# Four small moves in a hybrid layer's step: sums and turns one or two steps later, seven leading steps, tanh behind the turned weights

## The reference

```python
h = rms_norm(x, lw['norm_w'])
proj = jnp.einsum('bsd,de->bse', h, lw['w_in']) + lw['b_in']
(dn_qkv, dn_z, dn_b, dn_a, lru_x, lru_g, fq, fk, fv, ff, fg, mq, mg, mgate) = jnp.split(proj, IN_OFFSETS, axis=-1)
# A: gated DeltaNet (conv, l2 norms, per-head decay dn_a, beta dn_b, chunks of 64, gated norm)
# B: RG-LRU (conv, block-diagonal gates, scan)
# C: forgetting attention: 4 heads of 128, logits + c[t] - c[s], c = cumulative sum of log forget (ff), causal
# M: cross-attention into 256 memory tokens, 4 heads of 128, with normed q and k
# each branch -> D_MODEL, times sigmoid(mgate) of that branch, summed, output projection, + x
```

## Time and profile before

| | |
|---|---|
| median of 3 runs | 1656.29 us (1655.22 to 1657.52) |
| profiled execution, own time | 1660.77 us |
| its span | 1659.1 us |
| TensorE busy | 1604.7 us (97%) |
| VectorE busy | 886.6 us (53%) |
| ScalarE busy | 537.8 us (32%) |
| GpSimd busy | 507.3 us (31%) |
| mean granted clock of TensorE | 0.994 |

### The profile page before, as it was taken

One profiled execution on the slowest core, in us unless ns is written; L12 is line 12 of the kernel. 1 busy time (PEld: TensorE's weight loads), 2 busy tenths in 40 slices (PEclk: granted clock), 3 DMA queues, 4 the chain that ended last, 5 costly groups with the idle time before them and its releaser, 6 DMA issues. The chain is left out here.

```text
span 1659.1 us, 26024 instructions
## 1 busy us (share of the span) xinstructions
PE 1604.7 (97%) x10539; PEld 1538.3 (93%) x10539; DVE 886.6 (53%) x1291; ACT 537.8 (32%) x935; POOL 507.3 (31%) x382
## 2 busy tenths in 40 slices
PE   5999999999999999999999999999999999999998
PEld 4989999999999999999889889999989999889976
DVE  4678752444444442790486772444667552895611
ACT  6323343222222222233344442311145223654300
POOL 2433416334333312811344551222212221103400
PEclk9999999999999999999999999999999999999999
DMA  4212155222222114532276353135210332434521
GB/s 157 53 26 54 52 151 133 71 58 71 71 71 71 52 52 145 154 116 78 85 191 191 112 177 102 46 121 164 60 39 17 112 103 69 150 120 143 150 90 58
DMA packets 189365, 163.16 MB, mean 98 GB/s; under 512 B 18381, under 2 KB 157056, under 8 KB 188727
## 3 DMA queue, kind: packets, MB, share of 16 engines
q1 hardware_dynamic: 189246, 161.51, 34.0%
HBM read 131.38 MB, written 30.22 MB: 97 GB/s over the span
## 5 line engine op out<-in xcount | busy, mean ns | idle before, releaser
L276 POOL TENSOR_TENSOR wL<-w_raw,wH 128x1024 fp32r<-128x1024 f32 (+1 forms) x112 | 239.7, 2141 | 793.6 <-ACT wH L269 793.4
L335 PE MATMUL ps<-hH,wH 128*128 128x344 f32 x1920 | 457.7, 341 | 12.9 <-PEq L196 3.7
L335 PE MATMUL ps<-hL,wH 128*128 128x344 f32 x1920 | 420.2, 321 | 0.0
L335 PE MATMUL ps<-hH,wL 128*128 128x344 f32 x1920 | 418.9, 320 | 0.0
L335 PEld LDWEIGHTS ps<-hH,wH 128*128 128x128 f32 x1920 | 316.1, 190 | 27.0 <-issue 10.8
L335 PEld LDWEIGHTS ps<-hL,wH 128*128 128x128 f32 x1920 | 327.3, 189 | 0.2
L335 PEld LDWEIGHTS ps<-hH,wL 128*128 128x128 f32 x1920 | 324.7, 189 | 0.0
L269 ACT ACTIVATE wH<-w_raw 128x1024 fp32r<-128x1024 f32 (+1 forms) x116 | 108.5, 936 | 116.6 <-PE ps L335 107.0
L2944 POOL TENSOR_SCALAR fa_logits<-fox_c_bc,token_scalars 128x128 f32<-128x128 f32 (+7 forms) x32 | 60.2, 1882 | 51.2 <-DMA fox_c_bc<-rows_g_c_beta 29.5
L1906 ACT ACTIVATE d_m<-ps 128x512 f32<-128x512 f32 x48 | 28.7, 598 | 134.6 <-PE ps L2088 134.6
L1273 DVE SCALAR_TENSOR_TENSOR m_th<-m_th,ps 128x1032 f32<-128x1032 f32 x24 | 29.5, 1228 | 62.1 <-PE ps L335 57.4
(11 more groups left out here) (586 smaller groups left out, 2759.7 us busy)
## 6 DMA issues: line engine op xcount, KB each, us to landing
w_raw<-in_w_in SPq DMA_DIRECT2D x80, 512.0 KB, 5.2
m_th<-gate_spill SPq DMA_DIRECT2D x28, 516.0 KB, 4.3
gate_spill<-d_gate SPq DMA_DIRECT2D x18, 516.0 KB, 3.0
fa_kv<-in_cache_fox_k SPq DMA_DIRECT2D x32, 256.0 KB, 3.0
fa_kv<-in_cache_fox_v SPq DMA_DIRECT2D x32, 256.0 KB, 3.5
w_raw<-in_w_branch SPq DMA_DIRECT2D x32, 256.0 KB, 2.9
gate_spill<-fa_gate SPq DMA_DIRECT2D x10, 516.0 KB
x_rows<-in_x_prompt SPq DMA_DIRECT2D x8, 512.0 KB, 6.0
```

The source lines that it names most:

```text
L276: pool.tensor_tensor(self.wL[:, t % 2, 0:nk], self.raw_at(t)[:, 0:nk], self.wH[:, t % 2, 0:nk].bitcast(F32), ALU.subtract).then_inc(self.w ...
L335: last = pe.matmul(self.ps[:, b + g, 0:cols], w[:, t % 2, k], x[:, k, g * cols:(g + 1) * cols], start=(k == 0 and n == 0), stop=(k == nk - ...
```

## The change

It has four parts.

1. `SmallColumns.pe_step`: the running sums (L746, L747) go from ahead of step 1 of tile 6 to ahead of step 3, the transpose of the rows (L753) from step 5 to step 7.
2. `UnitFactors.pe_part`: the turn of the unit factors (L1620) goes from step 0 of part 1 to step 1, that of the decode tokens' q and k (L1626) from step 3 to step 4.
3. `attend`: `LEAD` is 7 instead of 6, in both attentions. The steps left over are 73 instead of 74 in the forgetting attention and 25 instead of 26 in the memory attention, dealt out over the same 64 parts.
4. `SiluBulk`: the tanh leaves `act` for a function of its own, `act_tanh`, which ACT comes to behind the unit's turned probabilities and the division and output of the units before. For the gate tiles of the forgetting attention this function is empty.

```diff
--- before.py
+++ after.py
@@ -759,9 +759,9 @@
             self.pe_logits(pe)
         if (j, k) == (5, 1):
             self.pe_turn(pe)
-        if (j, k) == (6, 1):
+        if (j, k) == (6, 3):
             self.pe_sums(pe)
-        if (j, k) == (6, 5):
+        if (j, k) == (6, 7):
             self.pe_rows(pe)
         if (j, k) == (8, 0):
             pe.wait_ge(self.N["out"], 1)
@@ -1615,11 +1615,11 @@
 
     def pe_part(self, pe, j, k):
         K, N = self.K, self.N
-        if (j, k) == (1, 0):
+        if (j, k) == (1, 1):
             pe.wait_ge(N["rn"], 1)
             pe.transpose(K.ps[0:self.N_SUMS, 7, 0:P], self.RB[:].rearrange("p r h t -> p (r h t)"), K.ident[:]
                          ).then_inc(N["tr"], 1)
-        if (j, k) == (1, 3):
+        if (j, k) == (1, 4):
             pe.wait_ge(N["moved"], 1)
             for r, x in enumerate((K.OT, K.merged)):
                 for h in range(H):
@@ -2726,6 +2726,8 @@
             act.wait_ge(self.spilled[q], 16 * (j // self.slots))
         K.evac_by_bank(act, t, self.GATE[:, q])
 
+    def act_tanh(self, act, t): pass
+
     def dve(self, dve, t): pass
 
     def sync(self, sp, t):
@@ -2752,6 +2754,9 @@
         b = BROW[self.name] + j
         act.activation(G[:, j].rearrange("p (a b) -> p a b", a=3), K.psum(t), ACT.Identity, scale=0.5,
                        bias=K.hbias[:, b:b + 1]).then_inc(K.evac_act, 1)
+
+    def act_tanh(self, act, t):
+        K, G, j = self.K, self.G, t - self.t0
         act.wait_ge(*K.emptied(t))
         if j >= 1:
             act.wait_ge(self.silu, j)
@@ -2783,7 +2788,7 @@
     its = [(h, t) for h in range(H) for t in range(TT8)]
     nb = [t + 1 if fox else MEM // P for _, t in its]
     NL = 3
-    LEAD = 6
+    LEAD = 7
 
     UB = 4 if fox else MEM // P
     units = [(n, b, min(UB, nb[n] - b)) for n in range(len(its)) for b in range(0, nb[n], UB)]
@@ -3273,6 +3278,8 @@
                         if u == of_tile[n][0]:
                             for t in ended_at[2 * n + 1]:
                                 bulk.act(act, t)
+                    for t in ended_at[2 * n] + ended_at[2 * n + 1]:
+                        bulk.act_tanh(act, t)
                     decode(n)
                     if n - 1 in ready_at:
                         branch.act_hi(act, ready_at[n - 1])
```

## The result

The changed kernel takes 1670.51 us (median of 4 runs, 1667.78 to 1672.09) against 1656.9 us for the kernel before (4 runs, 1655.22 to 1657.59): ratio 1.0074, 95% interval 1.0049 to 1.0099. The forecast was 1655.6 us, 0.7 faster.

What follows compares the result with a forecast made beforehand. TensorE, busy 1604.7 of 1659.1 us, was taken to bound the kernel. Terms -2.3 + 0.6 + 0 + 2.4 gave 0.7 us gained, 1655.6 us; own range 1653.2 to 1658.4, 8-in-10 range 1651.5 to 1659.8.

Steps and rivals of the forecast that it cites:

- Part 1, -2.3: Small columns: later rows delay SP's stores and weight load, stopping TensorE at the later L786; 2.3 us lost.
- Part 2, +0.6: Unit factors: the third L1737's wait goes, with L1613 undisturbed under the low part; 0.6 us gained, bounds 0.65 and -1.8.
- Part 3, forgetting attention, 0: Seventh leading step in the forgetting attention: gains and losses cancel to 0, bounds -3.2 and +1.5.
- the low part ahead of the fourth bias: Forgetting attention, GpSimd: third tile's low part delays unit 3's bias by 4.6 us, logits by 2.3; 0.9 lost net.
- the wait for the logits that I put at over 4: Forgetting attention, TensorE near 833 us: the wait for DVE's logits, 2.08 before, ends 2.3 us later.
- I gained 0.9 at 993.70: Forgetting attention: TensorE's idle of 0.73 for L312 goes as tile end and begin stand apart; 0.73 + 0.15 gained.
- Parts 3 and 4, memory attention, +2.4: Memory attention, leading step and moved tanh: 1.42 + 0.6 + 2.1 - 1.3, less 0.4 for collisions; 2.4 us gained, bounds 0 and 4.9.
- The two waits for the turned probabilities: Memory attention: with the tanh behind the copy, two TensorE waits of 1.46 fall to about 0.4 each; 2.1 us gained.
- The slow stretch behind the idle at L3048: Memory attention: clock at 0.50 for some 2.8 us around the filled 1.47 idle; half its cost, 0.6 us, counted as gained.
- The faster one: Rival: the weight load has slack and the memory attention gives all; 6.05 us gained, 1650.2 us; chance 0.20.
- The slower one: Rival: earlier low parts hold up L1613 at the unit factors and the fourth bias; -4.0 us, 1660.3 us; chance 0.15.
- Trading places: Rival: filled waits open again a step on and loads keep their times; 0 to 0.5 us either way, 1656.3; chance 0.15.

Runs made afterwards that it cites:

- p13_small_sp: Kernel before with the small columns' sums and rows two steps later and one more weight load ahead of the stores on SP: ratio 0.9992, -1.2 us at equal clock.
- p2_unit: Kernel before with only the unit factors' turns one step later: ratio 1.0011, -1.3 us at equal clock.
- p9_fox_pool: Kernel before with seven leading steps in the forgetting attention, GpSimd keeping its order of six: ratio 1.0027, +3.8 us at equal clock.
- p8_fox_sp: Kernel before with seven leading steps in the forgetting attention, SP keeping its order of six: ratio 1.0018, +3.1 us at equal clock.
- p10_fox_both: Kernel before with seven leading steps in the forgetting attention, SP and GpSimd both keeping their orders of six: ratio 1.0009, +2.3 us at equal clock.
- p12_fox_act: As p10_fox_both, with ScalarE taking a gate tile that ends in a unit's first half ahead of the next unit's exponential: ratio 1.0002, +2.4 us at equal clock.
- p5_mem_lead: Kernel before with seven leading steps in the memory attention, the tanh where it was: ratio 1.0009, +2.2 us at equal clock.
- p15_keep: Kernel before with seven leading steps in both attentions, the seventh taken from the first part, all tile borders unmoved: ratio 0.9999, -0.7 us at equal clock.
- p11_mem_dve: As p5_mem_lead, with VectorE's SiLU one unit later for tiles ending in a unit's second half: ratio 1.0010, +1.6 us at equal clock.
- p3_fox_lead: Kernel before with seven leading steps in the forgetting attention alone: ratio 1.0034, +5.5 us at equal clock.
- p1_small: Kernel before with only the small columns' sums and rows two steps later: ratio 1.0031, +3.0 us at equal clock.

## Why the prediction was wrong

One sum in it is off without touching the rest: the nine waits that it lists add up to 13.0 us, not 12.3. By its terms:

- **Part 1, -2.3.** The mechanism held, and its times from L786's 0.94 to the stop of 2.94, though SP's delay of 2.06 (forecast: 2.3) came about otherwise than I said. `p13_small_sp` shows that the load behind the stores is the whole of it. The size was 3.0 at equal clock, and some 2.3 more, with the wide interval above, go with the lower mean clock; in the one stretch that can be read, the clock added 1.5. I had priced the clock only where an idle would vanish, not where a new one arises.
- **Part 2, +0.6.** Right: 0.8 in the changed kernel's lag, 1.3 +- 0.85 in the times of `p2_unit`, with L1613 undisturbed. On top of `p13_small_sp` it adds nothing that can be told (0.0 +- 1.2).
- **Part 3, forgetting attention, 0.** This is the step that failed: 5.5 slower. Of its terms the low part ahead of the fourth bias was right in place, and worth 1.7 +- 1.2 (`p9_fox_pool`), where I had 0.9 net; the wait for the logits that I put at over 4 was 2.56. The step missing is SP. I followed the moved tile ends on GpSimd, ScalarE and TensorE, but not to the gate spill that SP issues at a tile's end. It stood behind unit 4's cache pages and now stands ahead of them, waits there for the tile, and holds up the pages and the next head's row of sums. `p8_fox_sp` puts it at 2.4 +- 1.2. The third piece, 2.3 that both queues leave, I had in small: I gained 0.9 at 993.70 and put 1.0 for one border, while the borders cost waits that change place (`p10_fox_both`, `p12_fox_act`).
- **Parts 3 and 4, memory attention, +2.4.** Wrong in sign: 1.9 slower. The two waits for the turned probabilities and the idle at L3048 went as I said. "For two of the four tiles the tanh comes about 1.3 later by ACT's order" was the wrong cause and half the size: VectorE's idle is 2.6 with the tanh in either place (`p5_mem_lead`), since the tile now ends in a unit's second half, behind the point at which VectorE turns to it. The tanh's move by itself gives 0.6 +- 0.85, where I had 2.1 for the two waits that it shortens. The slow stretch behind the idle at L3048 was 3.4 us long, not 2.8, and is gone in the changed kernel's trace, which has another at 1489.
- **The rivals.** The faster one fell on both counts: the load had no slack, and the memory attention lost. The slower one named a right mechanism, low parts that come sooner, and gave it the wrong place at the unit factors and a price of 4.0 in all. Trading places describes what the leading steps do once the borders are left alone (`p15_keep`). By my bounds the forgetting attention could lose at most 3.2 and the memory attention nothing; they lost 5.5 and 1.9. The forecast's own range took half of these bounds, as if the unknowns in them were independent; they all hang on one number, `LEAD`, which moves the nine borders of the one attention and the three of the other at once.

What stays open: how the 2.3 us of `p10_fox_both` and the 1.6 of `p11_mem_dve` divide over single waits; both are made of several under 1 us that shift from kernel to kernel.

## What to carry to other kernels

A constant that deals work out evenly moves every border when it changes by one. If an idle is to be filled, take the step from its neighbour and leave the rest where it is, then look at each engine's order, the DMA queue above all: an issue that waits for a tile's end blocks everything behind it, and one weight load issued behind thirteen small stores, and not ahead of them, turned a gain of 1.2 us into a loss of 3.0. And price a new stop of 2 to 3 us on TensorE at more than its length, for the granted clock may fall behind it.

## What the runs showed of the hardware

The granted clock falls to 0.50 for 3.4 or 6.8 us, once for 13.7, in two to six places of each profiled execution, the end aside. They come with stops of TensorE, but not with the same stop in each. Behind the first 60 us, the falls were before the change at 268, 763 and 1408 us; in `p2_unit`, whose edit lies around 200 to 220 us, at 217 and 831. Two windows of `p2_unit` and one of `p3_fox_lead`:

```profile
218.00:219.00 1.00, 1.00 (x5) 1.00 (x4) 1.00 (x1) 0.47 (x1) 0.67 (x1) 0.50 0.22 31
...
833.00:834.00 1.00, 1.00 (x4) 0.84 (x3) 1.00 (x2) 0.31 (x2) 0.00 (x0) 0.50 0.71 160
```

```profile
873.00:874.00 1.00, 1.00 (x5) 1.00 (x5) 1.00 (x1) 0.00 (x0) 0.00 (x0) 0.50 0.82 255
```

The stop of 2.1 us ahead of the second is in both kernels, and only in one of them the clock fell behind it; the third comes with the wait of 3.5 for `fa_gate`. So a stop gives a chance of a slow stretch. The 20 traces of this study say how large: of their 66 falls between 60 us and the end, each begins not over 2.4 us from the end of a stop of 1.4 us or more. It followed 9 of 63 stops of 1.4 to 1.6 us, 20 of 78 of 1.6 to 1.9, 29 of 43 of 1.9 to 2.2, 8 of 11 longer ones, and none of 44 of 1.0 to 1.4. The fall near 148 us is in the two traces that have the stop at the later L786 (`p1_small` and the changed kernel) and in no other. These stops stand in few places of much the same kernel, so what else about a place counts is not shown. The spread of 10 us between runs of one program goes with the clock, by the slope above. The Trainium skill (TensorE: Matmul & The Clock Gate, "What's actually happening") says that the throttled level is the default, that activity lifts it, and that what watches the activity runs on its own, not from the kernel's start, so that the same kernel differs from run to run. The trace agrees, with falls that change place, and so do the mean clocks of the kernel before, 0.990 to 1.000 over its 159 runs. By its words I should have priced any new stop of this length as a chance, and not only the one that I filled.

A VectorE operation on two operands in SBUF was stretched beside GpSimd's low part (L1118 2.19 us, 1.23 alone at 214.04 in the same trace), while L1613, with its input in PSUM, took 1.28 under it, as it does alone. That is what the Trainium skill says of the shared port (SBUF — State Buffer, "Who interferes with whom"), and here it decided the sign of a term.
